# Two weight groups behind a layer norm read the scaled residual; mean, root and bias come in at the eviction

## The reference, cut to what matters

```python
def layer_norm(x, g, b):
    mu = jnp.mean(xf, axis=-1, keepdims=True)
    var = jnp.mean(jnp.square(xf - mu), axis=-1, keepdims=True)
    y = (xf - mu) * lax.rsqrt(var + LN_EPS) * g + b
...
h = layer_norm(ALPHA * h + 0.5 * swiglu(h, ffn1...), ln_gain[l, 0], ln_bias[l, 0])
mix = short_conv(h, ...)                  # layer 0: bgate, cgate, val = split(h @ w_in)
mix = forgetting_attention(h, ...)        # layer 1
h = layer_norm(ALPHA * h + mix, ln_gain[l, 1], ln_bias[l, 1])
h = layer_norm(ALPHA * h + 0.5 * swiglu(h, ffn2...), ln_gain[l, 2], ln_bias[l, 2])
```

## Time and profile before

| what | before |
|---|---|
| median of 3 runs | 1621.33 us (1621.05 to 1621.41) |
| span of the profiled execution, first to last instruction | 1618.6 us |
| TensorE's matmuls busy | 1593.4 us, 98% |
| VectorE busy | 1126.9 us, 70% |
| ScalarE busy | 927.6 us, 57% |
| mean granted clock of TensorE | 0.999 |
| moved by DMA | 266.52 MB, mean 165 GB/s |

### The profile page before, as it was taken

One profiled execution on the slowest core, in us unless ns is written; L12 is line 12 of the kernel. 1 busy time (PEld: TensorE's weight loads), 2 busy tenths in 40 slices (PEclk: granted clock), 3 DMA queues, 4 the chain that ended last, 5 costly groups with the idle time before them and its releaser, 6 DMA issues.

```text
span 1618.6 us, 31076 instructions
## 1 busy us (share of the span) xinstructions
PE 1593.4 (98%) x12574; PEld 1541.5 (95%) x12574; DVE 1126.9 (70%) x2417; ACT 927.6 (57%) x2028; POOL 167.1 (10%) x156
## 2 busy tenths in 40 slices
PE   9999999999999999999999999999999999999998
PEld 9999999999999999999999999988899889999987
DVE  7555578787755887566468775686639997788962
ACT  5444355474444764456456553466666887567652
POOL 4000000000000000000110000102342653100000
PEclk9999999999999999999999999999999999999999
DMA  9554555555555555554255555753354335555551
GB/s 292 170 182 153 187 159 181 157 180 162 173 171 175 182 174 166 188 184 143 67 183 160 183 177 185 198 163 105 105 158 156 106 104 183 183 195 183 183 177 58
DMA packets 251391, 266.52 MB, mean 165 GB/s; under 512 B 4763, under 2 KB 246753, under 8 KB 251248
## 3 DMA queue, kind: packets, MB, share of 16 engines
q1 hardware_dynamic: 249600, 260.72, 50.7%
q0 software_dynamic: 1648, 3.81, 0.9%
HBM read 263.42 MB, written 1.09 MB: 163 GB/s over the span
## 4 chain that ended last, share of the span: by engine, by line
PE 88%; DVE 6%; ACT 4%; issue 1%; DMA 0%; POOL 0%; SPq 0%; DVEq 0%; ACTq 0%
PE ps L1040 52%; PE ps L1042 26%; DVE wl L2217 2%; PE ps L1000 1%; PE ps L999 1%; PE ps L1001 1%; ACT wh L1509 1%; PE ps L776 1%; PE ps L809 0%; PE ps L793 0%; DVE CY L2183 0%; DVE R L1830 0%; DMA X<-in_meta 0%; DVE XC L1790 0%; ACT SP L1313 0%
## 5 line engine op out<-in xcount | busy, mean ns | idle before, releaser
L2217 DVE TENSOR_TENSOR wl<-raw,wh 128x512 fp32r<-128x512 f32 (+1 forms) x968 | 641.0, 711 | 299.5 <-ACT wh L1509 293.9
L1509 ACT ACTIVATE wh<-raw 128x512 fp32r<-128x512 f32 (+1 forms) x1004 | 552.1, 611 | 192.2 <-PE ps L1040 168.6
L1040 PE MATMUL ps<-XH,wh 128*128 128x258 f32 (+3 forms) x2464 | 618.1, 287 | 4.0 <-ACT XH L1134 3.5
L1042 PE MATMUL ps<-XH,wl 128*128 128x258 f32 (+3 forms) x2464 | 614.4, 286 | 0.0
L1040 PEld LDWEIGHTS ps<-XH,wh 128*128 128x128 f32 x2464 | 466.6, 189 | 7.9 <-issue 6.7
L1042 PEld LDWEIGHTS ps<-XH,wl 128*128 128x128 f32 x2464 | 465.8, 189 | 0.1
L1040 PE MATMUL ps<-XL,wh 128*128 128x258 f32 (+3 forms) x2464 | 334.6, 287 | 0.0
L1040 PEld LDWEIGHTS ps<-XL,wh 128*128 128x128 f32 x2464 | 315.9, 190 | 1.4 <-issue 0.7
L1042 PE MATMUL ps<-HH,wl 128*128 128x272 f32 (+1 forms) x704 | 173.4, 284 | 0.0
L1040 PE MATMUL ps<-HH,wh 128*128 128x272 f32 (+1 forms) x704 | 173.4, 285 | 0.0
L1042 PEld LDWEIGHTS ps<-HH,wl 128*128 128x128 f32 x704 | 132.5, 188 | 0.0
(11 more groups left out here) (447 smaller groups left out, 2070.6 us busy)
## 6 DMA issues: line engine op xcount, KB each, us to landing
raw<-in_ffn_wg SPq DMA_DIRECT2D x44, 1024.0 KB, 5.4
raw<-in_ffn_wu SPq DMA_DIRECT2D x44, 1024.0 KB, 5.4
raw<-in_w_in SPq DMA_DIRECT2D x33, 1024.0 KB, 5.3
raw<-in_ffn_wd SPq DMA_DIRECT2D x32, 1024.0 KB, 5.3
raw<-in_w_ffn_in SPq DMA_DIRECT2D x22, 1024.0 KB, 5.1
raw<-in_ffn_wd SPq DMA_DIRECT2D x16, 768.0 KB, 4.6
...
```

What stands on the lines that cost most here:

```text
L1040: mm = e.matmul(o, hi[:, k, c], xk, start=begin, stop=stop)
L1042: e.matmul(o, lo[:, k, c], xk, start=False, stop=False)
L1509: e.activation(wh[u.n % NH][:, c], raw[u.n % NR][:, c], ACT.Copy).then_inc(s_hi, 1)
L2217: e.tensor_tensor(wl[u.n % NR][:, c], raw[u.n % NR][:, c], wh[u.n % NH][:, c].bitcast(F32), ALU.subtract).then_inc(s_lo, 1)
```

## The change

Behind norms 0, 1, 2 and 4 the first two weight groups read KXH and KXL, the two parts of gain x R: not centred, not divided by the deviation. Chunks 0 to 5 of them are made during the last groups of the projection (`act_raw`, `dve_raw`), 6 and 7 in the norm's first side step. LNV is summed over all eight chunks, the three mean matmuls become one, and it moves to the second side step, as the centring does. The columns T, T+1 of KXH hold gain and bias, so that a group's extra PSUM columns give the weighted sums of both; the eviction (`rooted_raw`) multiplies by RS, adds -mean x RS times the gain column (`raw_mean`, NMR) and then the bias as before. XH and XL are made later, for the third group on. The credits of the steps change from rate 4 and 0.01 to rate 4.4 and -0.7. The 18 warming matmuls go. The postponed quarters in `vector` stay where they are, behind the first side step. The diff, without semaphore numbers that only shift and without the places where the bias is read from PR in place of PB:

```diff
@@ -257,7 +258,8 @@
         SQB = sb(st, "SQB", [128, 2, T])
-    KXH, KXL = sb(b1, "KXH", [128, KD, T], F32R), sb(b1, "KXL", [128, KD, T], F32R)
+    KXHW, KXLW = sb(b1, "KXH", [128, KD, T + 2], F32R), sb(b1, "KXL", [128, KD, T + 2], F32R)
+    KXH, KXL = KXHW[:, :, 0:T], KXLW[:, :, 0:T]
     T2 = [SQ[:, 3, :], R[:, 7, :]]
...
@@ -464,7 +467,7 @@
         P.run(("ln", i), 1)
-        P.rate, P.credit = 4, 0.01
+        P.rate, P.credit = 4.4, -0.7
...
@@ -593,14 +596,18 @@
+    RAW, CEN = {0: 8, 1: 24, 2: 40, 4: 72}, {0: 16, 1: 32, 2: 48, 4: 80}
...
+    x_raw = {i: Xs(KXHW, KXLW, s_xh, s_xl, RAW[i], n0, T + 2) for i, n0 in ((0, 0), (1, 0), (2, NMETA), (4, NMETA))}
...
@@ -617,9 +624,7 @@
         mean = PS[7][:, n0:T]
-        if i == 0:
-            e.wait_ge(s_xl, 8)
-        e.wait_ge(s_ls, 5 * i + 5)
+        e.wait_ge(s_ls, LS0[i] + 5)
         e.matmul(mean, mean1[:], LNV[:, n0:T], start=True, stop=False)
...
@@ -628,15 +633,14 @@
-        if i == 4:
-            e.wait_ge(s_s2, 8)
-            pe_warm(e, 8, KXH[:, 0, :], 4)
-        pe_mean(e, i, n0)
-        if i == 4:
-            pe_warm(e, 10, KXH[:, 0, :], 4)
+        yield
+        if i == 0:
+            e.wait_ge(s_xl, 8)
+        e.wait_ge(s_ls, LS0[i] + 7)
+        e.matmul(PS[7][:, n0:T], mean1[:], LNV[:, n0:T], start=True, stop=True).then_inc(s_mu, 1)
         yield
         late = 2 if i == 4 else 0
-        yield from idle(4 + 3 + late)
+        yield from idle(6 + late)
         e.wait_ge(s_qa, 4 * i + 4)
...
@@ -1056,7 +1060,8 @@
             for j in range(11):
-                gemms([("gate", f, j), ("up", f, j)], x, j == 0)
+                first = f and j == 0
+                gemms([("gate", f, j), ("up", f, j)], x_raw[(0, 1, 2, 4)[f]] if first else x, j == (1 if f else 0) or first)
                 if f and j == 0:
...
@@ -1076,10 +1081,10 @@
         for j in range(4):
-            gemms([("c", j), ("v", j)], x_conv, j == 0)
+            gemms([("c", j), ("v", j)], x_conv if j else x_raw[0], j == 0)
             if j == 0:
                 side.run(at["rs", 0])
-            gemms([("b", j)], x_conv, False)
+            gemms([("b", j)], x_conv, j == 0)
         gemms([("conv_out", j) for j in range(4)], x_ch)
...
@@ -1124,22 +1129,42 @@
+    def bias_cols(i):
+        t, r0 = col["ln_bias"]
+        return PV[:, t, r0 + 8 * i:r0 + 8 * i + 8].unsqueeze(2).to_broadcast([128, KD, 2])
+    def gain_bias_cols(i):
+        t, r0 = col["ln_gain"]
+        return PV[:, t, r0:r0 + 96].rearrange("p (a n) -> p n a", a=2)[:, 8 * i:8 * i + 8, :]
+    def act_raw(e, i, n0, pair):
+        for k in (2 * pair, 2 * pair + 1):
+            e.wait_ge(s_res, 8 * i + k + 1)
+            if k == 0:
+                e.activation(KXHW[:, :, T:T + 2], gain_bias_cols(i), ACT.Copy)
+                e.activation(XHW[:, :, T:T + 2], bias_cols(i), ACT.Copy)
+            e.activation(KXH[:, k, n0:T], R[:, k, n0:T], ACT.Copy, scale=pc("ln_gain", 8 * i + k)).then_inc(s_xh, 1)
     def act_norm(e, i, n0, hi=None):
...
-        t, r0 = col["ln_bias"]
-        e.wait_ge(s_ls, 5 * i + 1)
-        e.activation(XHW[:, :, T:T + 2], PV[:, t, r0 + 8 * i:r0 + 8 * i + 8].unsqueeze(2).to_broadcast([128, KD, 2]), ACT.Copy)
-        for k in range(KD):
-            e.wait_ge(s_cen, 5 * i + (1, 2, 3, 3, 4, 4, 5, 5)[k])
-            e.activation(XH[:, k, n0:T], XC[:, k, n0:T], ACT.Copy, scale=pc("ln_gain", 8 * i + k)).then_inc(s_xh, 1)
+        act_raw(e, i, n0, 3)
         yield
...
             for k in range(2 * j, 2 * j + 2, w):
+                e.wait_ge(s_cen, 5 * i + (1, 2, 3, 3, 4, 4, 5, 5)[k])
                 e.activation(R[:, k:k + w, n0:T], XC[:, k:k + w, n0:T], ACT.Square).then_inc(s_sq, 1)
-            yield
-        yield from idle(4)
+            if j in (1, 3):
+                yield
+        for k in range(KD):
+            e.activation(XH[:, k, n0:T], XC[:, k, n0:T], ACT.Copy, scale=pc("ln_gain", 8 * i + k)).then_inc(s_xh, 1)
+            if k in (3, 7):
+                yield
+        yield from idle(2)
         e.preload_act_table_set("natural_log_exp_and_others")
+        yield
+        yield
         e.wait_ge(s_var, var_done[i])
...
@@ -1562,6 +1587,8 @@
                 group(("down", f, j))
+                if j and f != 2 and f != 3:
+                    act_raw(e, (0, 2)[f], n0, j - 1)
                 side.run(groups["down", f, j].after)
...
@@ -1652,6 +1681,8 @@
             group(("ob", j))
+            if j:
+                act_raw(e, 4, NMETA, j - 1)
             side.run(groups["ob", j].after)
...
@@ -1781,8 +1812,20 @@
+    def dve_raw(e, i, n0, pair):
+        for k in (2 * pair, 2 * pair + 1):
+            e.wait_ge(s_xh, RAW[i] + k + 1)
+            if k == 0:
+                e.tensor_tensor(KXLW[:, :, T:T + 2], gain_bias_cols(i), KXHW[:, :, T:T + 2].bitcast(F32), ALU.subtract)
+            e.scalar_tensor_tensor(out=KXL[:, k, n0:T], in0=R[:, k, n0:T], scalar=pc("ln_gain", 8 * i + k),
+                                   in1=KXH[:, k, n0:T].bitcast(F32), op0=ALU.mult, op1=ALU.subtract).then_inc(s_xl, 1)
     def dve_norm(e, i, n0, lo=None):
-        t, r0 = col["ln_bias"]
+        dve_raw(e, i, n0, 3)
+        yield
+        if lo is not None:
+            e.memset(WFS[:].bitcast(F32), 0.0).then_inc(s_wfz, 1)
         e.wait_ge(s_mu, i + 1)
...
@@ -1790,20 +1833,19 @@
                                 ALU.subtract).then_inc(s_cen, 1)
+        yield
+        yield from idle(2)
+        dve_square_sum(e, R, n0, s_sq, 5 * i, 4 * i)
+        yield
         for k in range(KD):
-            e.wait_ge(s_xh, (8, 16, 24, 40, 48)[i] + k + 1)
+            e.wait_ge(s_xh, CEN[i] + k + 1)
             if k == 0:
-                e.tensor_tensor(XLW[:, :, T:T + 2],
-                                PV[:, t, r0 + 8 * i:r0 + 8 * i + 8].unsqueeze(2).to_broadcast([128, KD, 2]),
-                                XHW[:, :, T:T + 2].bitcast(F32), ALU.subtract)
+                e.tensor_tensor(XLW[:, :, T:T + 2], bias_cols(i), XHW[:, :, T:T + 2].bitcast(F32), ALU.subtract)
             e.scalar_tensor_tensor(out=XL[:, k, n0:T], in0=XC[:, k, n0:T], scalar=pc("ln_gain", 8 * i + k),
                                    in1=XH[:, k, n0:T].bitcast(F32), op0=ALU.mult, op1=ALU.subtract).then_inc(s_xl, 1)
-        yield
-        if lo is not None:
-            e.memset(WFS[:].bitcast(F32), 0.0).then_inc(s_wfz, 1)
-        yield from idle(4)
-        dve_square_sum(e, R, n0, s_sq, 5 * i, 4 * i)
-        yield from idle(4 + 1)
+            if k in (3, 7):
+                yield
+        yield from idle(3)
         e.wait_ge(s_rs, i + 1)
...
@@ -2230,9 +2272,32 @@
+        def raw_mean(i, n0):
+            e.wait_ge(s_rs, i + 1)
+            e.scalar_tensor_tensor(out=NMR[:, 0:T - n0], in0=PS[7][:, n0:T], scalar=-1.0, in1=RS[:, 0:T - n0],
+                                   op0=ALU.mult, op1=ALU.mult).then_inc(s_nmr, 1)
+        def rooted_raw(dsts, G, c, i, s):
+            n = dsts[0].shape[-1]
+            for m, dst in enumerate(dsts):
+                e.wait_ge(s_acc, G.acc + m + 1)
+                e.tensor_copy(PR[:, 2 * (c + m):2 * (c + m) + 2], PS[G.b0 + m][:, n:n + 2])
+                e.tensor_tensor(dst, PS[G.b0 + m][:, 0:n], RS[:, 0:n], ALU.mult).then_inc(s_rt, 1)
+            r = (0, 1, 2, 2, 3)[i]
+            e.wait_ge(s_nmr, r + 1)
+            for m, dst in enumerate(dsts):
+                e.wait_ge(s_rt, 4 * r + c + m + 1)
+                e.scalar_tensor_tensor(out=dst, in0=NMR[:, 0:n], scalar=PR[:, 2 * (c + m):2 * (c + m) + 1], in1=dst,
+                                       op0=ALU.mult, op1=ALU.add).then_inc(s, 1)
         def ffn(f, n0, h_done):
...
                 sg, G = SG[f][j % 2], groups["gate", f, j]
+                if f and j == 0:
+                    rooted_raw([sg[:, m, n0:T] for m in range(2)], G, 0, (0, 1, 2, 4)[f], s_fr)
+                    return
                 for m in range(2):
...
@@ -2246,12 +2311,15 @@
                     side.run(at["rs", (0, 1, 2, 4)[f]])
-                    e.wait_ge(s_rs, (0, 1, 2, 4)[f] + 1)
+                    raw_mean((0, 1, 2, 4)[f], n0)
                     gate(j)
+                    rooted_raw([T2[m][:, n0:T] for m in range(2)], G, 2, (0, 1, 2, 4)[f], s_fr)
                 p = 4 * (j % 2) + 2
...
                     e.wait_ge(s_acc, G.acc + m + 1)
-                    if f:
+                    if late:
+                        pass
+                    elif f:
                         rooted(T2[m][:, n0:T], G, m, p + m, s_fr)
...
@@ -2282,13 +2353,13 @@
                                            in1=PS[b][:, c0:c0 + T - n0], op0=ALU.mult, op1=ALU.add).then_inc(s_res, 1)
-                if j < 3:
+                if j < 3 or i in RAW:
                     for k in (2 * j, 2 * j + 1):
...
                         if k > 1:
-                            e.wait_ge(s_ls, 5 * i + k - 1)
+                            e.wait_ge(s_ls, LS0[i] + k - 1)
```

(13 more changed lines are left out.)

56 lines of the change are left out of this document (33 added, 23 removed).

## The result

The changed kernel takes 1632.3 us (median of 4 runs, 1631.48 to 1632.62) against 1621.37 us (1621.05 to 1621.52) for the kernel before on the same chip: ratio 1.0069, 95% interval 1.0057 to 1.0081. It is slower by 10.9 us. I had said +3.0 (1624.4, range to 1627.0).

A forecast was written before the change was run, and what follows sets the result against it. TensorE, busy 98% of the span, was taken as the bound. Norm terms -0.5, -0.5, +0.2 and +3.8 gave +3.0 us, so 1621.33 + 3.04 = 1624.4 us; range 1617.5 to 1627.

The forecast's parts named there:

- my +3.0: Sum over the four norms: -0.5 at norms 0 and 1 each, +0.2 at norm 2, +3.8 at norm 4.
- rival (a): At the norms: VectorE's order does not bind, the gaps go; 11.7 us gained, 1610 us; chance 5%.
- the 0.3 us of variance waits: At the norms: variance waits that would go along with the gaps and the 0.93 us wait, within 11.7 us gained.
- Later groups hold: Behind the norms: VectorE's backlog of 4.5 us fits before later groups' evictions, so nothing is lost there.
- Rival (c): The clock falls behind waits that no bank wait covers: 1.7 us each, once or twice, 1626 to 1628; chance 15%.
- My argument for norm 4: Behind norm 4's 3.0 us wait, what the clock slows ends (867.5) before the banks come free: no term added.

## Why the prediction was wrong

**Durations, order, norms: right.** The first groups start on time. The variance waits 0.94, 0.94, 2.06 and 2.86 (said 1.2, 1.2, 2 and 3), the fourth group 0.42, 0.43, 0.71 and 2.06 (said 0.8, 0.8, 0.9, 1 or more), norm 4's centring starts 9.7 us behind the last OL matmul, as said. The corrections follow each other by 0.41. The norms give +2.7 for my +3.0, norm by norm, so that is no luck. That XH in front of H0 makes the variance wait, L3 the fourth group, and the postponed splits norm 4's centring, is shown by the kernels in which each was moved (the first two at norm 1). XL was not moved; that it holds the fourth group too is read from VectorE's order in the trace. One number of rival (a) is in no row: the 0.3 us of variance waits beside norm 4's 0.93. Before, norm 2's is 0.13 and those of norms 0 and 1 are nothing.

**The step that failed** is "Later groups hold: in norm 0 VectorE comes to the third group's eviction at 242.5 where the banks are wanted at 246.5, and each wl is three groups ahead; its backlog of 4.5 us fits." I compared the backlog with one deadline, the next one, and with the kind of deadline that comes back each group. It fits there. But nothing works the backlog off: VectorE's idle time before (waits of 4.0 in 45 us in the convolution, of 12.5 in 85 in FFN 2) is waiting for ScalarE, which waits for VectorE, so both come late together and the idle time is no room. The backlog is still 4.9 us forty microseconds later, where a deadline of another kind stands: the last input of a matmul series (CH), and the last side step of a chain (CTT). The room was 2.4 us at the one, 1.5 at the other. The sum put this term at nothing; it measured 7.7 us, 2.2 at CH and 5.5 at CTT. The trace of before showed where to look: VectorE's first wait for TensorE behind norm 0 is at 283.60, and in FFN 2 there is none before 625. Behind norm 1 the first is at 365.85 before and 392.15 after, 26 us later, and no such deadline lies between; that this is why norm 1 alone loses nothing is argued from the trace, and the kernel with norm 1 alone agrees (nothing lost behind the norm).

**The clock.** Rival (c) had the mechanism and the price for one fall (1.7 us), but at the norms. It struck at CTT, for 3.1 us, and in other kernels' profiles at the end of the convolution (1.5 to 2.7) and at norms 2 and 4. My argument for norm 4, that what the low clock slows ends before the banks come free, held: in the kernel with norm 4 alone the clock was 0.50 over 6 us behind the variance wait, and the loss was 3.9 in place of 3.7. It does not cover the bank wait itself: where the clock fell behind that one it cost 1.7 (the centring moved) and 1.5 us (the transposes' wait filled).

**What stays open.** Why the clock falls behind one wait and not behind another of the same length: it stayed at 1.00 behind 2.86 and 2.06 us at norm 4 in the changed kernel, and fell behind 1.62 at CTT; at the convolution's end it stayed behind 1.94 us in one profile and fell behind 2.0 in another. How much of VectorE's later work ScalarE alone would let it win back is not separated: no kernel took work from both. That TensorE could take the transposes a side step later was not tried on the chip, nor the change at norm 2 with such an order.
